# Dilated attention by residues modulo 4, with its products in quarters of the array

## The reference

```python
DSW_GROUPS = ((128, 1), (512, 4), (2048, 16))      # window, dilation; 8 heads of 64 in each group
qkv = (h @ w_qkv).reshape(B, S, 3, G, Hg, HEAD_DIM)
q = rmsnorm(qkv[:, :, 0], q_gain); k = rmsnorm(qkv[:, :, 1], k_gain); v = qkv[:, :, 2]
# query t of group g attends to t - dilation*i, i = 0..window/dilation, with a bias by distance;
# outputs of the three groups are weighted by the softmax of their log-sum-exps
return o.astype(h.dtype) @ w_o                     # 512 -> 1024
```

## Time and profile before

| what | value |
|---|---|
| median of 3 runs | 881.75 us (880.66 to 882.27) |
| profiled execution | 881.07 us |
| its span, first to last instruction | 879.3 us |
| PE busy | 872.3 us, 99% |
| DVE busy | 620.3 us, 71% |
| ACT busy | 491.8 us, 56% |
| POOL busy | 40.4 us, 5% |
| DMA | 155.54 MB, mean 177 GB/s |

### The profile page before, as it was taken

How to read it: one execution, slowest core, us unless ns; L and a number is a source line. 1 busy time by engine, 2 the same in 40 slices (tenths; PEclk the granted TensorE clock), 3 DMA queues, 4 the chain that set the end, 5 groups by cost and what they waited for, 6 DMA issues and landing times.

```text
span 879.3 us, 13709 instructions
## 1 busy us (share of the span) xinstructions
PE 872.3 (99%) x5546; PEld 750.9 (85%) x5546; DVE 620.3 (71%) x1064; ACT 491.8 (56%) x742; POOL 40.4 (5%) x69
## 2 busy tenths in 40 slices
PE   9999999999999999999999999999999999999998
PEld 8887888987888888878999988888777899998886
DVE  5889987989988987776666644466778586664441
ACT  7566836667847654576555533355667565553330
POOL 1700010000000000100000000010000000000000
PEclk9999999999999999999999999999999999999999
DMA  8963254642344678623655556555553386555540
GB/s 300 314 257 106 97 192 149 240 145 97 110 163 160 239 242 226 182 70 131 191 184 187 183 203 193 197 186 189 168 168 120 97 282 195 187 186 192 171 152 25
DMA packets 79454, 155.54 MB, mean 177 GB/s; under 512 B 5644, under 2 KB 7852, under 8 KB 79392
## 3 DMA queue, kind: packets, MB, share of 16 engines
q1 hardware_dynamic: 75200, 142.81, 48.2%
q0 software_dynamic: 4192, 11.86, 5.1%
HBM read 153.55 MB, written 1.11 MB: 176 GB/s over the span
## 4 chain that ended last, share of the span: by engine, by line
PE 90%; ACT 4%; DVE 3%; issue 2%; DMA 1%; ACTq 0%; DVEq 0%
PE ps L810 18%; PE ps L812 17%; PE ps L811 17%; PE ps L841 9%; PE ps L842 9%; PE ps L843 9%; PE ps_mid L758 3%; DVE w_lo L1964 1%; ACT w_hi L1465 1%; PE ps_mid L1004 1%; PE ps L758 1%; PE ps_mid L1034 1%; PE ps_mid L810 1%; ACT y_tok L1599 1%; DMA w_raw<-in_w_in 1%
## 5 line engine op out<-in xcount | busy, mean ns | idle before, releaser
L1964 DVE TENSOR_TENSOR w_lo<-w_raw,w_hi 128x2048 fp32r<-128x2048 f32 x133 | 299.8, 2260 | 143.7 <-ACT w_hi L1465 143.5
L1465 ACT ACTIVATE w_hi<-w_raw 128x2048 fp32r<-128x2048 f32 x133 | 250.9, 1891 | 192.2 <-PE ps L812 141.5
L810 PE MATMUL ps<-w_hi,act_hi 128*128 128x512 f32 (+1 forms) x446 | 177.6, 398 | 1.3 <-ACT area L1485 0.9
L812 PE MATMUL ps<-w_hi,act_lo 128*128 128x512 f32 (+1 forms) x446 | 171.1, 384 | 0.0
L811 PE MATMUL ps<-w_lo,act_hi 128*128 128x512 f32 (+1 forms) x446 | 170.8, 383 | 0.0
L810 PE MATMUL ps<-w_hi,hid 128*128 128x512 f32 x296 | 116.1, 392 | 0.0
L812 PE MATMUL ps<-w_hi,hid 128*128 128x512 f32 x296 | 115.2, 389 | 0.0
L811 PE MATMUL ps<-w_lo,hid 128*128 128x512 f32 x296 | 115.2, 389 | 0.0
L841 PE MATMUL ps<-act_hi,w_hi 128*128 128x256 f32 x384 | 109.9, 286 | 0.0
L843 PE MATMUL ps<-act_hi,w_lo 128*128 128x256 f32 x384 | 107.6, 280 | 0.0
L842 PE MATMUL ps<-act_lo,w_hi 128*128 128x256 f32 x384 | 107.6, 280 | 0.0
(11 more groups left out here) (354 smaller groups left out, 1202.1 us busy)
## 6 DMA issues: line engine op xcount, KB each, us to landing
w_raw<-in_ffn_w SPq DMA_DIRECT2D x64, 1024.0 KB, 5.2
w_raw<-in_w_in SPq DMA_DIRECT2D x21, 1024.0 KB, 6.0
w_raw<-in_a_w_qkv SPq DMA_DIRECT2D x18, 1024.0 KB, 4.8
w_raw<-in_b_w_qkv SPq DMA_DIRECT2D x12, 1024.0 KB, 5.0
w_raw<-in_w_out SPq DMA_DIRECT2D x8, 1024.0 KB, 4.8
w_raw<-in_b_w_o SPq DMA_DIRECT2D x4, 1024.0 KB, 5.0
w_raw<-in_w_in SPq DMA_DIRECT2D x12, 256.0 KB, 5.6
w_raw<-in_w_in SPq DMA_DIRECT2D x4, 512.0 KB, 3.5
```

Source lines behind the costliest of these rows:

```text
L810: pe.matmul(o, ah, wh, start=first, stop=False)
L812: mm = pe.matmul(o, al, wh, start=False, stop=last)
L1465: act.activation(w_hi[:, c % RING, :, 0:n], w_raw[:, c % RAW, :, 0:n], ACT.Copy).then_inc(w_hi_done, 1)
L1964: dve.tensor_tensor(lo, w_raw[:, c % RAW, :, 0:n], hi.bitcast(F), ALU.subtract).then_inc(w_lo_done, 1)
```

## The change

Queries, keys and values of groups 1 and 2 are handled by the token's residue modulo 4. A token is 4 i + 2 r + t, with t and r either 0 or 1 and i from 0 to 63. A score tile t now has 128 queries: partition half r holds the 64 queries of residue 2 r + t. For group 0 ("near") such a tile has all 256 keys; for groups 1 and 2 ("far") only the 64 keys of the same residue each. Every product of the scores has 64 partitions and 64 stationary columns, a quarter of the array, and there are 8 near ones of 256 columns and 16 far ones of 64 columns for a pair. The far scores of the two groups are interleaved column by column. A head's scores are 768 columns in two tiles of 384, each tile in a bank of its own.

The turned weights of a pair are three banks of four turns each (near of each head, far of both heads) instead of six of three. The near output is 8 products of 128 columns for a pair, the far output 16 of 64 columns in quarters. All four pairs' outputs stand in two banks, and their high and low parts are written back to token order with a step of four elements.

So that the values of groups 1 and 2 come out in residue order, the activations of blocks f+7 and f+8 are copied once into that order (`mixed_high` on ScalarE, `mixed_low` on VectorE, 2048 columns each), and the tokens' scale factors too, through DRAM (`rstd_row`, three small DMAs). Each head's bias comes by six DMAs instead of one. ScalarE has `softmax(2)` and `softmax(3)` ahead of both evictions of the last block; VectorE has all of `logits(2)` to `logits(6)` nearly together.

```diff
 def dil_weights(u):
+    return dil_P[:, u % 6, :].rearrange("p (t n) -> p t n", t=2)
+def dil_scores(e, t):
+    return ps_mid[:, 1024 * e + 512 * t:1024 * e + 512 * t + 384]
+def near_scores(e, t):
+    return dil_scores(e, t)[:, 128 * t:128 * t + 256]
+def far_scores(e, t, g):
+    at = 255 + g - 256 * t
+    return dil_scores(e, t)[:, at:at + 127:2]
+MIXED_LO = 14848
+def mixed_acts(k):
+    lo = MIXED_LO + 256 * k
+    return tables_turn[:, 256 * k:256 * k + 256], hid_flat[:, lo:lo + 256] if k < 6 else early_room[:, 256 * k - 1536:256 * k - 1280]
+def dil_turned(n):
+    return dil_PT[n % 6]
+def mixed_sums(p):
+    return ps_mid[:, 2048:3072].rearrange("p (t n) -> p t n", t=2)[:, :, 128 * p:128 * p + 128].rearrange("p t (r i) -> p t r i", r=2)
+def token_order(v):
+    return v.rearrange("p (i r t) -> p t r i", t=2, r=2)
...
+        with nc.allow_non_contiguous_dma(reason="one element per partition"):
+            pool.wait_ge(rstd_done, 1)
+            pool.dma_start(bass.AP(rstd_row.tensor, 0, [[1, 128], [128, 2]]), rstd[:, 0, :]).then_inc(rstd_out, 16)
+            pool.wait_ge(rstd_out, 16)
+            for t in range(2):
+                pool.dma_start(rstd_mixed[64 * t:64 * t + 64, :], bass.AP(rstd_row.tensor, t, [[4, 64], [2, 2]])).then_inc(rstd_in, 16)
...
+                for r in range(2):
+                    rows = bias_of(u)[64 * r:64 * r + 64]
+                    near = bass.AP(bias_vec.tensor, u * 1152 + 2 * r, [[4, 64], [1, 2], [1, S]])
+                    pool.dma_start(rows[:, 128:640].rearrange("p (t n) -> p t n", t=2), near).then_inc(bias_in[u % 4], 16)
+                    far = bass.AP(bias_vec.tensor, u * 1152 + 896, [[2, 64], [1, 128]])
+                    for at in (0, 640):
+                        pool.dma_start(rows[:, at:at + 128], far).then_inc(bias_in[u % 4], 16)
             else:
+                src = bass.AP(bias_vec.tensor, (u - DSW_HEADS) * 1152 + 512, [[1, 128], [1, S]])
+                pool.dma_start(bias_of(u), src).then_inc(bias_in[u % 4], 16)
...
+            if b == FIRST["dsw"] + 7 and half == 0 and k == 0:
+                pe.wait_ge(mixed_hi_done, 1)
+                pe.wait_ge(mixed_lo_done, 1)
...
+            elif b in (FIRST["dsw"] + 7, FIRST["dsw"] + 8):
+                ah, al = [v[:, 128 * half:128 * half + 128] for v in mixed_acts(k)]
             else:
...
+        row = lambda e: slice(64 * e, 64 * e + 64)
+        q = lambda e, g, i: qkv[row(e), p % 2, 512 * g + 256 * (p // 2) + i:512 * g + 256 * (p // 2) + 253 + i:4]
+        k = lambda e, g, i: qkv[row(e), p % 2, 1536 + 512 * g + 256 * (p // 2) + i:1789 + 512 * g + 256 * (p // 2) + i:4]
+        keys = lambda e: qkv[row(e), p % 2, 1536 + 256 * (p // 2):1792 + 256 * (p // 2)]
+        for t in range(2):
+            for r in range(2):
+                for e in range(2):
+                    pe.matmul(near_scores(e, t)[row(r)], q(e, 0, 2 * r + t), keys(e), start=True, stop=True)
+        for t in range(2):
+            for g in (1, 2):
+                for r in range(2):
+                    for e in range(2):
+                        i = 2 * r + t
+                        mm = pe.matmul(far_scores(e, t, g)[row(r)], q(e, g, i), k(e, g, i), start=True, stop=True)
+        mm.then_inc(s_ready, 2)
...
+    def dil_transposes(n):
+        p, part = n // 3, n % 3
+        bank = t_bank(2, n, 0)
+        if part < 2:
+            pe.wait_ge(p_scaled, UNIT0[2] + 2 * p + part + 1)
+        if n >= 2:
+            turned_out(n - 2)
+        if part < 2:
+            for chunk in range(2):
+                for t in range(2):
+                    mm = turn(bank, 256 * chunk + 128 * t, dil_weights_turn(2 * p + part, 0, t, chunk))
+        else:
             for e in range(2):
+                for g in (1, 2):
+                    mm = turn(bank, 256 * e + 128 * (g - 1), dil_weights_turn(2 * p + e, g, None))
         mm.then_inc(t_ready, 1)
+    def dil_near_output(p):
+        if p:
             pe.wait_ge(pair_lo, p)
+        turned_out(3 * p)
+        turned_out(3 * p + 1)
+        for chunk in range(2):
+            for t in range(2):
+                for e in range(2):
+                    c0 = 512 * 6 + 64 * (2 * p + e)
+                    pe.matmul(ps_mid[64 * e:64 * e + 64, 2048 + 512 * t + 128 * p:2176 + 512 * t + 128 * p],
+                              qkv[:, chunk, c0:c0 + 64], dil_turned(3 * p + e)[:, 256 * chunk + 128 * t:256 * chunk + 128 * t + 128],
+                              start=chunk == 0, stop=False)
+    def dil_far_output(p):
+        turned_out(3 * p + 2)
+        pt = dil_turned(3 * p + 2)
+        for g in (1, 2):
+            for r in range(2):
+                for t in range(2):
+                    for e in range(2):
+                        c0 = 512 * (6 + g) + 64 * (2 * p + e)
+                        at = 2048 + 512 * t + 128 * p + 64 * r
+                        mm = pe.matmul(ps_mid[64 * e:64 * e + 64, at:at + 64], qkv[64 * t:64 * t + 64, r, c0:c0 + 64],
+                                       pt[64 * t:64 * t + 64, 256 * e + 128 * (g - 1) + 64 * r:256 * e + 128 * (g - 1) + 64 * r + 64],
+                                       start=False, stop=g == 2 and r == 1)
+        mm.then_inc(pair_ps, 1)
     def dilated():
...
             pass
         pe.wait_ge(acc_free[0], free_count(o))
+        dil_transposes(0)
         dil_pair_scores(2)
         pe.wait_ge(acc_free[1], free_count(o))
+        dil_transposes(1)
+        dil_transposes(2)
+        dil_near_output(0)
+        dil_transposes(3)
+        dil_pair_scores(3)
+        dil_far_output(0)
+        dil_transposes(4)
+        dil_transposes(5)
+        dil_transposes(6)
+        dil_near_output(1)
+        dil_far_output(1)
+        dil_transposes(7)
+        dil_transposes(8)
+        tokens(o, 0, (0,))
         tokens(o, 1, (0,))
+        dil_near_output(2)
+        dil_transposes(9)
+        dil_far_output(2)
+        dil_transposes(10)
+        dil_transposes(11)
         tokens(o, 0, (1,))
         tokens(o, 1, (1,))
+        dil_near_output(3)
+        dil_far_output(3)
         for half in range(2):
             tokens(o, half, (2,))
...
+    def mixed_high():
+        act.activation(tables_turn[:, 0:2048].rearrange("p (k r i) -> p k r i", r=4, i=64),
+                       act_hi.rearrange("p k (i r) -> p k r i", r=4), ACT.Copy).then_inc(mixed_hi_done, 1)
     def dil_high(p):
         act.wait_ge(pair_ps, p + 1)
+        act.activation(token_order(act_hi[:, p, :]), mixed_sums(p), ACT.Copy).then_inc(pair_hi, 1)
...
+            for t in range(2):
+                ins = act.activation(p[:, t], p[:, t], ACT.Exp, bias=m[:, t:t + 1], scale=-1.0, accum_out=dn[:, t:t + 1])
+            ins.then_inc(p_ready, 1)
+        def transposed(n):
+            act.wait_ge(t_ready, PCH0[2] + n + 1)
+            act.activation(dil_turned(n), t_bank(2, n, 0), ACT.Copy).then_inc(pt_a, 1)
...
         softmax(0)
         softmax(1)
         splits(f + 8, 0)
+        softmax(2)
+        softmax(3)
         take(f + 8, 0)
         take(f + 8, 1)
+        transposed(0)
         softmax(4)
         softmax(5)
+        transposed(2)
+        transposed(3)
         dil_high(0)
+        transposed(5)
         softmax(6)
+        transposed(6)
         dil_high(1)
         softmax(7)
+        transposed(8)
+        transposed(9)
         dil_high(2)
+        transposed(11)
         dil_high(3)
         splits(f + 8, 1)
...
+                if i == 3:
+                    mixed_low()
                 continue
             for half in range(2):
...
+    def mixed_low():
+        dve.tensor_copy(hid_flat[:, MIXED_LO:MIXED_LO + 1536].rearrange("p (k r i) -> p k r i", r=4, i=64),
+                        act_lo[:, 0:6].rearrange("p k (i r) -> p k r i", r=4))
+        dve.tensor_copy(early_room[:, 0:512].rearrange("p (k r i) -> p k r i", r=4, i=64),
+                        act_lo[:, 6:8].rearrange("p k (i r) -> p k r i", r=4)).then_inc(mixed_lo_done, 1)
     def dil_low(p):
         dve.wait_ge(pair_hi, p + 1)
-        dve.tensor_tensor(act_lo[:, p, :], ps7[:, S * (p % 2):S * (p % 2) + S], act_hi[:, p, :].bitcast(F), ALU.subtract).then_inc(pair_lo, 1)
+        dve.tensor_tensor(token_order(act_lo[:, p, :]), mixed_sums(p), token_order(act_hi[:, p, :]).bitcast(F), ALU.subtract).then_inc(pair_lo, 1)
...
+                dve.wait_ge(t_ready, PCH0[2] + 3)
+            dve.wait_ge(bias_in[u % 4], 96 * (u // 4 + 1))
+            for t in range(2):
+                ins = dve.tensor_tensor_reduce(out=dil_weights(u)[:, t], in0=dil_scores(u % 2, t),
+                                               in1=spread(bias_of(u)[:, 384 * t + 383:384 * t + 384], [(-1, 384)]), scale=-1.0, scalar=3.0e38,
+                                               op0=ALU.add, op1=ALU.min, accum_out=ttr[:, u % 4, t:t + 1])
             ins.then_inc(ttr_done, 1)
...
+            for t in range(2):
+                ins = dve.tensor_scalar(p[:, t], p[:, t], r[:, t:t + 1], None, ALU.mult)
```

(11 more changed lines are left out.)

235 lines of the change are left out of this document (58 added, 177 removed).

## The result

The changed kernel is slower: 894.58 us (median of 4 runs, 892.73 to 895.43) against 882.01 (4 runs, 880.66 to 883.08), which is 12.6 us by the medians. The ratio on record is 1.0132 with a 95% interval of 1.0113 to 1.0150, or 10.0 to 13.2 us; it is not the quotient of the two medians (1.0142). The forecast was 877.7, with a range of 875.0 to 885.2. The profiled execution took 892.73 us, 11.7 more than that of before.

The account below looks back on a forecast made before the run. TensorE, busy for 99% of the span, was taken as the bound. Cheaper scores, outputs and turns, less waits, put the third output tile at 395.52 against 398.94: 881.07 - 3.4 = 877.7 us, range 875.0 to 885.2.

Parts of the forecast that it names:

- The row vector through DRAM: Ahead of the folds: two hops at 6.2 us, needed some 40 us later, so cost put at nothing.
- The weight queue's lead of three chunks: Weight ring: every chunk has a lead of about three chunks of 5.4 us, hiding the push from `mixed_low`.
- The dilated stretch: Scores, turns and outputs on TensorE, followed to the third output tile: 3.4 us earlier than before.
- the third tile: First product of the third output tile, `tokens(o, 0, (2,))`: to start at 395.52 against 398.94.
- The waits: TensorE waits about 1 us before the first turn, 1.90 before near_output(0), 1.04 before turns(6).
- the far rows of the scores: 64-column score rows on TensorE, 32 a pair, taken at 22 ns each; a whole pair 1.86 us.
- the turns: Turns on TensorE at 0.10 us each, 48 instead of 72: 2.4 us less.
- The far output: Far output groups on TensorE: 32 rows of 64 columns, 0.70 and 0.10 for the shape, 0.80 us.
- The 0.6 us gained on the first two pairs: First two score pairs save 0.30 us each; lost again as TensorE waits for ScalarE, softmax(2) and (3) preceding evictions.
- Quarters: Rival: quarters run two, not four, at once; scores 3.1 us a pair, third tile 1.0 later, 882.0; chance 0.15.
- Strided operands: Rival: steps of four and two halve the score products; a pair 4.1 us, end 4.1 later, 885.2; chance 0.18.
- A hand-over of 1.30: Rival: a head's logits on VectorE take 1.30 instead of 0.96; 1.5 earlier instead of 3.4, 879.6; chance 0.12.

Follow-up runs that it names:

- experiment 2: Kernel before with only the three small row-vector DMAs added, fold copies behind them, and the 8-byte tile declared; 892.90 us, 1.0110.
- experiment 7: Kernel before with only the row vector's store (256 elements of 4 B) and fold copies behind it, 8-byte tile declared; 894.16 us, 1.0131.
- experiment 12: Changed kernel with the row vector kept behind the bias vectors in one DRAM tensor, the three DMAs unchanged; 892.06 us, 1.0110.
- experiment 18: Changed kernel with only the filler tile `to_line` cut by 24 B more, undoing the 32 B shift; 889.41 us, 1.0079.
- experiment 1: Changed kernel without the three row-vector DMAs and the wait, mixed blocks scaled in token order (values wrong); 887.85 us, 1.0052.
- experiment 13: Kernel before with the changed kernel's 8-byte tile `rstd_mixed` and two semaphores declared, unused; 886.40 us, 1.0041.
- experiment 17: Kernel of experiment 10 with the filler tile `to_line` cut by 24 B more, undoing the 32 B shift; 878.25 us, 0.9953.
- experiment 3: Changed kernel with the scale factors reordered on the chip by eight TensorE products instead of through DRAM; 886.62 us, 1.0048.
- experiment 10: Kernel of experiment 8 without the now unused 1 KB DRAM tensor `rstd_row`; 881.34 us, 0.9993.
- experiment 4: Kernel of experiment 3 with ScalarE's evictions back ahead of softmax(2) and softmax(3), and ScalarE copying the second turned bank; 883.09 us, 1.0004.
- experiment 8: Kernel of experiment 4 with head 4's scaling ahead of head 6's logits on VectorE; 881.98 us, 0.9991.

## Why the prediction was wrong, step by step

- **The row vector through DRAM, put at nothing: the step that failed.** I reckoned its own latency (two hops at 6.2 us against a need 40 us later), and that held: it was never waited for. What failed is the price: I took the row of a 384 KB bias load in the earlier trace rows for a DMA of 256 elements of 4 B, and asked only who waits for it, not whom it holds up. The weight queue's lead of three chunks did not cover 9.8 us. Between the two anchors it cost 8.9 us in the changed kernel's profile, 6.5 to 8.7 in those of experiments 2, 7, 12 and 18; on the whole time, by experiments 1, 2 and 7 with the 3.7 of experiment 13 taken from the last two, 6 to 8.
- **What was not on the list: the room of `rstd_mixed`.** The change cuts `to_line` from 144 to 142, which I read as keeping the place. It moved all tiles behind it, by 32 B if rooms are rounded as above: 3.7 us in the kernel before (experiment 13), 3.1 in the best one (17), 5.2 in the changed one (18). No row of before could price it; the line's name could have warned.
- **The dilated stretch, 3.4 us forecast: 1.1 came at the third tile.** From copy to third tile it was 52.84 us before and 51.77 after. The waits were as forecast (0.80, 1.78 and 1.22 for about 1, 1.90 and 1.04). Mis-sized were the far rows of the scores (33 ns from start to start for 22, 0.35 us a pair), the turns (0.116 for 0.10, 0.8 us in all) and the clock, which I kept at 1.00 through waits that I had forecast myself: near output 1.33 for 1.06 and the fourth pair's scores 2.73 for 2.03, some 1.1 us. The far output, 0.63, was cheaper than the 0.80 forecast. The 1.1 us were then given back: the residual's first turn came 6.06 us behind the third tile instead of 5.46, and the end 481.4 instead of 480.4.
- **The order was the loss I had seen and accepted** ("The 0.6 us gained on the first two pairs is given back here"). With it undone and head 4 scaled first, copy to end is 528.2 to 528.4 against 533.2: 5.0 us, more than forecast. The work removed from TensorE was real.
- **The rivals.** Quarters do run four at once: near rows took 61 ns. Strided operands cost 15 ns a far row and not the near 40 that the slower case needed. A hand-over of 1.30 for a head's logits did not come: 0.96 as forecast. "That it does not do what it says" was put aside with the words that the row vector's lateness was inside the other cases. That the kernel got slower is no hit for the 0.19 given to it: the time is 9 us above the range, and it came by a mechanism that stood among the nothings and in none of the rivals.
- **Hidden as forecast:** the two copies, though ScalarE's took twice its price, and the bias DMAs, landed after 3.4 to 4.2 us with no wait on them. ScalarE's high part and VectorE's low part:

```profile
324.27 3.96 ACT L1730 ACTIVATE tables_turn<-act_hi 128x2048 fp32r<-128x2048 f32 x1
```
```profile
327.16 1.58 DVE L2377 CAST hid<-act_lo 128x1536 fp32r<-128x1536 f32 x1
328.64 0.64 DVE L2379 CAST early_acts<-act_lo 128x512 fp32r<-128x512 f32 x1
```

Put together for the changed kernel: +12.6 us measured; some 7 the store, 4 to 5 the shift, and a dilated stretch that gained next to nothing. Whether the two costs add or feed each other isn't settled: the same filler edit gave 3.1 us in experiment 17 and 5.2 in 18, and the intervals of the ratios are too wide to tell these apart. Open stays how a shift of 32 B slows the transfers near 40 us, and which of the moved tiles and which multiple (64 B or a larger one) matter, since only this one shift was run. The half-clock stretches in part of the executions stand behind waits where a profile caught them: behind the early wait in experiments 1, 3 and 10, behind the 1.16 us wait in experiment 4, where an early wait of 2.05 us was followed by none. For the executions that were not profiled it stays an inference.

## What to carry to other kernels

Look at a DMA's elements as well as its bytes, and ask whom it holds up on the other queues, not only who waits for it: 256 values of 4 B cost some 7 us here, and eight tiny products did the same turn for 0.6. A new tile, however small, can move all that lie behind it; here that cost 3 to 5 us, so keep the large ones where they were before comparing two kernels. And where TensorE's work shrinks, put the engines that feed it back in the order that lets it start: what its waits cost was their length and the half clock behind them.

## What the runs showed that was not expected

- With the SBUF tiles shifted by 32 B, the loads issued near 40 us are slower: 259 against 351 GB/s from 40 to 46, loads of 512 KB landing after 12.0 instead of 10.2 us and of 32 KB after 8.2 instead of 6.3. Other stretches are not (390 GB/s from 50 to 54).
- A store of 256 elements of 4 B lands after 8.2 to 9.8 us, of 128 elements of 8 B after 5.3, of one after 3.0; during the first, all DMA traffic of the core falls to 29 GB/s from 295 to 300, while ScalarE waits for a chunk.
- With fp32 operands in steps of four elements a 64-column row cost TensorE 35 ns against 20 (32 rows in 1.13 and 0.64 us); ScalarE's copy with such a step took 3.96 us where a plain 2048-column one takes 1.9; VectorE's took 2.2, no more than the 2.3 forecast for a plain one.
- Behind waits of 0.80 and 1.78 us, TensorE's granted clock was 0.50 from 392 to 395; behind the 1.16 us of experiment 4 its turns ran at 1.30 for 1.10 us; behind the 0.31 us of experiment 8 it stayed at 1.00.
